# Last attention: moving the value products of a head to other places in TensorE's written order

## What is computed

```python
def mla_mixer(h, positions, w_in, q_g, kv_g, w_uq, w_ukv, w_out):
    cq, ckv, kr = jnp.split(h @ w_in, [Q_LORA, Q_LORA + KV_LORA], axis=-1)
    q = (rms_norm_2(cq, q_g) @ w_uq).reshape(bsz, seq, C_HEADS, C_NOPE + C_ROPE)
    kv = (rms_norm_2(ckv, kv_g) @ w_ukv).reshape(bsz, seq, C_HEADS, C_NOPE + C_V)
    ...
    def attend(qblk):
        s = jnp.einsum("bqhd,bkhd->bhqk", qblk, kf, preferred_element_type=jnp.float32) * scale
        pr = jax.nn.softmax(s, axis=-1)
        return jnp.einsum("bhqk,bkhd->bqhd", pr.astype(v.dtype), v)
    o = lax.map(attend, qb)
    ...
    return o @ w_out
```

## Time and profile before

| what | value |
|---|---|
| median of 3 runs | 2099.23 us (2098.19 to 2099.62) |
| the profiled execution | 2095.59 us |
| its span, first to last instruction | 2093.8 us |
| mean granted TensorE clock | 0.963 |
| TensorE busy | 1924.4 us, 92% |
| VectorE busy | 1168.8 us, 56% |
| ScalarE busy | 719.1 us, 34% |
| the loop over heads of the last attention | 1525.9 to 1681.6 us |

### The profile page before, as it was taken

How to read it: one execution, slowest core, us unless ns; L and a number is a source line. 1 busy time by engine, 2 the same in 40 slices (tenths; PEclk the granted TensorE clock), 3 DMA queues, 4 the chain that set the end, 5 groups by cost and what they waited for, 6 DMA issues and landing times. The chain is left out here.

```text
span 2093.8 us, 24983 instructions
## 1 busy us (share of the span) xinstructions
PE 1924.4 (92%) x9036; PEld 1575.8 (75%) x9036; DVE 1168.8 (56%) x1681; ACT 719.1 (34%) x1017; POOL 98.8 (5%) x105
## 2 busy tenths in 40 slices
PE   4998799889999997896789999999999999999997
PEld 2787577667887876674568888888788888888886
DVE  4556664566474666976645343447677644343444
ACT  3235222333242334432324232334344433232232
POOL 1020000200000002000000000000321100000000
PEclk9999799899999998898889999999999999999998
DMA  4223201122323332221013333332210123333333
GB/s 153 81 63 117 73 1 58 64 81 90 100 91 98 94 105 71 81 91 51 0 44 95 98 101 92 100 96 94 81 41 21 31 71 91 97 95 100 93 98 110
DMA packets 47237, 168.00 MB, mean 80 GB/s; under 512 B 5040, under 2 KB 5040, under 8 KB 47024
## 3 DMA queue, kind: packets, MB, share of 16 engines
q1 hardware_dynamic: 44352, 159.40, 24.7%
q10 hardware_dynamic: 2800, 7.45, 1.0%
HBM read 164.74 MB, written 2.10 MB: 80 GB/s over the span
## 5 line engine op out<-in xcount | busy, mean ns | idle before, releaser
L1107 ACT ACTIVATE w_hi<-raw 128x1024 fp32r<-128x1024 f32 x297 | 314.4, 1059 | 914.7 <-PE ps L479 913.9
L477 PE MATMUL ps<-h_hi,w_hi 128*128 128x512 f32 (+1 forms) x1376 | 553.0, 402 | 49.1 <-DVE w_lo L1603 35.6
L478 PE MATMUL ps<-h_lo,w_hi 128*128 128x512 f32 (+1 forms) x1376 | 541.8, 394 | 0.0
L479 PE MATMUL ps<-h_hi,w_lo 128*128 128x512 f32 (+1 forms) x1376 | 541.5, 394 | 0.0
L1603 DVE TENSOR_TENSOR w_lo<-raw,w_hi 128x1024 fp32r<-128x1024 f32 x297 | 364.7, 1229 | 194.4 <-ACT w_hi L1107 184.8
L477 PEld LDWEIGHTS ps<-h_hi,w_hi 128*128 128x128 f32 (+1 forms) x1376 | 262.0, 190 | 116.8 <-DVE w_lo L1603 31.6
L478 PEld LDWEIGHTS ps<-h_lo,w_hi 128*128 128x128 f32 (+1 forms) x1376 | 262.1, 191 | 56.2 <-issue 2.4
L479 PEld LDWEIGHTS ps<-h_hi,w_lo 128*128 128x128 f32 (+1 forms) x1376 | 261.3, 190 | 56.7
L477 PE MATMUL ps<-hid_hi,w_hi 128*128 128x512 f32 x688 | 268.6, 390 | 5.6 <-DVE hid_lo L2084 5.6
L479 PE MATMUL ps<-hid_hi,w_lo 128*128 128x512 f32 x688 | 268.4, 390 | 0.0
L478 PE MATMUL ps<-hid_lo,w_hi 128*128 128x512 f32 x688 | 268.3, 390 | 0.0
(11 more groups left out here) (353 smaller groups left out, 2209.9 us busy)
## 6 DMA issues: line engine op xcount, KB each, us to landing
raw<-in_panels SPq DMA_DIRECT2D x300, 512.0 KB, 3.6
x_in<-in_x ACTq DMA_DIRECT2D x1, 2048.0 KB, 16.6
x<-in_x ACTq DMA_DIRECT2D x1, 2048.0 KB, 8.5
out<-y SPq DMA_DIRECT2D x8, 256.0 KB, 2.0
first<-in_first ACTq DMA_DIRECT2D x1, 1568.0 KB, 19.9
second<-in_second ACTq DMA_DIRECT2D x1, 768.0 KB, 4.3
small<-in_small ACTq DMA_DIRECT2D x1, 332.0 KB, 5.1
masks<-in_masks ACTq DMA_DIRECT2D x1, 256.0 KB, 6.9
```

The source lines that it names most:

```text
L477: nc.tensor.matmul(out, a[0], b[0], start=start, stop=False)
L478: nc.tensor.matmul(out, a[0], b[1], start=False, stop=False)
L479: return nc.tensor.matmul(out, a[1], b[0], start=False, stop=stop)
L1107: nc.scalar.activation(w_hi[:, panel % 2, :], raw[:, panel % 4, :], ACT.Copy).then_inc(w_hi_ready, 1)
```

## The change

In TensorE's program alone, the four `values` calls of a head move. v0 goes from ahead of maxima 2 and 3 to behind `project_k`. v1 follows it at once, now ahead of `turn_pair`. v2 goes from behind `turn` (and `project_quad`) into the next head, behind that head's maxima 0 and 1 and right ahead of v'3. For the last head v2 stands behind the loop. No call is added or removed, no wait is changed, and the programs of the other engines stay as they are.

```diff
@@ -1068,25 +1068,26 @@
             if more:
                 maxima(n + 1, range(0, 2))
             if n:
+                values(n - 1, 2)
                 values(n - 1, 3)
             scores(n, 1)
             if even and p + 1 < PAIRS:
                 project_nope(p + 1)
-            values(n, 0)
             if more:
                 maxima(n + 1, range(2, 4))
             scores(n, 2)
             if even and p + 1 < PAIRS:
                 project_k(p + 1)
+            values(n, 0)
+            values(n, 1)
             if not even and p:
                 turn_pair(p - 1)
-            values(n, 1)
             scores(n, 3)
             if more:
                 turn(n + 1)
             if n % 4 == 1 and p + 2 < PAIRS:
                 project_quad(p // 2 + 1)
-            values(n, 2)
+        values(HEADS - 1, 2)
         values(HEADS - 1, 3)
         turn_pair(PAIRS - 1)
```

## The result

| | before | after |
|---|---|---|
| median | 2097.76 us (6 runs) | 2106.99 us (6 runs, 2105.24 to 2107.74) |
| ratio, 95% interval | | 1.0043 (1.0033 to 1.0054) |
| profiled execution, span | 2095.59, 2093.8 us | 2105.70, 2103.9 us |
| loop over heads | 155.68 us | 165.68 us |

The change makes the kernel slower by 9.2 us. The prediction was 2110.0 us, +10.8, with a range of 2105 to 2115. It was right in sign and size; the price was set a little too high.

The account below looks back on a forecast made before the run. TensorE's order was taken to bound the loop. Twelve emptied stretches of 0.90 us gave +10.8 us, all other terms 0; added to the median of 2099.23 us that made 2110.0 us, range 2105 to 2115.

Parts of the forecast that it names:

- The bound and the place: In the loop over heads TensorE's order is the bound, busy 153.32 of 155.70 us; nothing outside the loop should change.
- The stretch: Turn to scores 0 stays 1.25 us through VectorE; twelve heads lose v2's 0.90 us, three rotary ones nothing.
- The size: Whole execution slower by 10.8 us, from 12 x 0.90 in the loop; bounds 7.6 to 14.5.
- the pairs: 31 new pairs of value groups cost 0; bounds 2.8 us saved to 2.2 us lost.
- the handover of 0.07: At each boundary inside a merged pair of value groups, at worst 0.07 us lost, 2.2 us in all.
- the bound of 0.09 a pair: Each merged pair saves at best one late scores pass of 0.09 us, 2.8 us over 31 pairs.
- The slack of the turn: Between maxima 2, 3 and the turn, the negated maxima's slack grows from 1.18 to 2.1 us, winning nothing.
- The maxima behind a rotary projection: In three heads maxima 2, 3 come 0.90 us sooner against VectorE's reductions; taken as 0, at most 0.9 us in all.
- The signs to look for: Loop about 166.5 us, L477 load waits 14.5 us in 13 entries, ScalarE's waits for scores growing about as much as the loop.
- The round trip: Rival: turn to scores 0 shortens without v2; 0.35 to 0.9 us, within 0.2%, chance 0.06; shorter still, faster, 0.04.
- Pairs don't win 10.8 us: Rival: moving v0 and v1 wins back 10.8 us, needing 0.35 for each of 31 pairs; no separate chance given.
- The clock: Rival: idle gaps behind twelve turns lower TensorE's clock in the loop, 19 us more, 2129 us; chance 0.03.

Follow-up runs that it names:

- doubled shift: Changed kernel with VectorE's spreading of the shift done twice, only the second signalling: 2130.61 us, ratio 1.0154.
- half group: Changed kernel with two of v2's four matmuls back behind the turn, the other two in the next head: 2104.33 us, ratio 1.0031.
- v0 and v1 alone: Kernel before with only v0 and v1 moved together behind project_k, v2 left behind the turn: 2097.09 us, ratio 0.9995.
- the kernel with v0 in its old place: Kernel before with v1 and v2 both behind the turn, v0 still ahead of maxima 2 and 3: 2093.69 us, ratio 0.9980.
- v2 only: Kernel before with only v2 moved into the next head, v0 and v1 in their old places: 2109.97 us, ratio 1.0056.
- v2 before turn: Kernel before with v2 written ahead of the turn instead of behind it, in the same head: 2107.53 us, ratio 1.0048.
- shift twice, before: Kernel before with VectorE's spreading of the shift done twice: 2105.27 us, ratio 1.0040.
- the kernel with two groups and the doubled shift: Kernel with v1 and v2 behind the turn, v0 behind project_k, and VectorE's shift done twice: 2097.14 us, ratio 0.9996 against the kernel before.

## Why the prediction was right

*The bound and the place.* TensorE's order was the bound, its work unchanged, and nothing outside the loop moved (412.20 against 412.15 us). Right.

*The stretch.* Twelve stretches of 1.25 us with nothing in them, three with a rotary projection at 2.2 without idle time; the prediction had 2.11, since it counted v2's late second pass to the stretch, where it lies behind its end. Right. The row that the prediction rested it on, the first turn, was weaker than it took it for. It names GpSimd as the releaser of the scores, and GpSimd's copy ends at 1525.92, just when the scores start, so the 1.25 us could have been GpSimd's. The doubled shift settles it: the same first turn then takes 1.97 us, and GpSimd is done at 1527.98, 0.7 ahead of the scores. First the kernel before, then the doubled shift in the changed kernel:

```profile
1524.64 1.28 POOL L451 CAST q_lo<-quad_lo 32x512 fp32r<-32x512 f32 x2
...
1526.70 1.28 POOL L451 CAST q_lo<-quad_lo 32x512 fp32r<-32x512 f32 x2
1526.72 0.27 PE L726 MATMUL ps<-small,mla_negm 128*4 128x128 f32 x1
...
1528.69 0.47 PE L477 MATMUL ps<-q_hi,k_hi 128*128 128x512 f32 x1 [1.70 <-DVE q_hi L2061]
```

The swap of v2 and the turn, the half group and the doubled shift each confirm one side of it: what is in it, how much, and how long it is.

*The size.* 10.8 predicted, 10.00 in the loop and 9.2 in the median, whose interval (6.9 to 11.3 us) holds both. The term that was mis-sized is that of the pairs, taken at 0. v0 and v1 together measured -0.40 us for sixteen pairs. v2 alone, with its fifteen pairs, cost 10.64, only 0.16 less than 10.8, so the pairs don't all save alike. Both make 10.24, and 10.00 was measured. Of the last 0.24, 0.16 is a wait that the run with v0 and v1 alone has and the changed kernel has not: its maxima 2 and 3 of head 1, at 1541.18, are drawn over 0.78 us instead of 0.62. The sixteen passes themselves are no cheaper (0.112 each, as read). They are drawn over 1.89 us, where the old pair had 1.95 because its second group waited for an exponential; so the handover of 0.07 in the upper bound doesn't exist. What the 0.40 us are I didn't isolate; they lie within the bound of 0.09 a pair that the prediction had given.

*The slack of the turn.* The prediction said that negated maxima would be ready 2.1 us ahead of their turn instead of 1.18. That holds in odd heads from 3 on (ready at 1606.12, turn at 1608.16), not in even ones:

```profile
1576.03 0.17 DVE L2055 TENSOR_SCALAR mla_negm<-mla_mx 128x4 f32<-128x4 f32 x1
```

Its end, 1576.20, is only 1.14 ahead of the turn at 1577.34. In even heads VectorE's reductions queue behind its lowering of the projected queries, and that waits for the projection, which now ends later against the maxima. The wrong step cost nothing here. The waits of the turn in the kernel with v0 in its old place are something else: they are in heads with no projection between maxima and turn.

*The maxima behind a rotary projection.* They start at 1594.19, 7.86 us behind the turn (7.82 predicted), and the reductions that they need end at 1594.11:

```profile
1592.83 1.28 DVE L2051 TENSOR_REDUCE mla_mx<-ps 128x1 f32<-128x512 f32 x2
...
1594.19 0.62 PE L721 MATMUL ps<-k_hi,q_hi 128*128 128x512 f32 x2
```

Just in time; no wait of L721 for L2051 stands in the table. Right.

*The signs to look for.* The load's idle time is 17.7 us, not 14.5: the load for the turn runs 0.23 ahead of the turn's matmul, so each gap is drawn as 1.36 and not 1.1. That ScalarE's waits for scores would grow with the loop was wrong; they read 63.1 us in 46 waits against 67.7 in 61, since in odd heads the copy of the turned pair (line 1304) now stands in front of an exponential and takes over part of the wait (13.6 us in 8, where it had 2.6 in 1). The run with v0 and v1 alone shows the same 13.6 us.

*The rivals.* The round trip isn't shorter when it is empty: excluded by the 1.25. Pairs don't win 10.8 us: v0 and v1 together won 0.40. The clock stayed at 1.00 in the loops of all three profiled kernels with this length of idle time (the changed kernel, v2 only, v2 before turn).

## What to carry to other kernels

Where an in-order engine sends something through another engine and waits for it, write independent work of at least the round trip's length between the sending and the wait; 1.25 us here held one group of 0.9, and two groups took away the last 0.33. The round trip can be read in the trace at a place where nothing stands in it, such as the first one ahead of the loop, if nothing else could have released it at that moment. When a piece is moved away from such a place to be next to its like, its whole length is lost there, and hardly anything is gained where it goes (0.40 us for sixteen pairs here).

## What the runs showed of the hardware

TensorE's clock stood a row of short idle times in some of these kernels and not in others. With 1.15 us idle in twelve of the heads it was granted 2.4 GHz throughout the loop, in all three profiled kernels that have these stretches, and so it was with about 1.0 us idle in a round trip of 1.96 us (shift twice, before). With 1.86 us idle in the same twelve places it fell to 1.2 GHz six times in the loop, and that cost 15.7 us beside the 8.5 of the longer waits themselves. Outside the loop shorter idle times were followed by a fall as well: 0.72 us in the half group and 0.74 us in the kernel with two groups and the doubled shift, while the changed kernel stood idle for 0.72 us at the first of these places and kept its clock. What decides there the runs don't show. A rule of the Trainium skill ("TensorE: Matmul & The Clock Gate", section "A second HAM failure mode: psum-queue depth-cycling") says that short idles between groups can make the clock swing. The traces disagree for the 1.15 us idles in the loop and agree for the 1.86 us ones.
